# Splitting the gates of a delta rule's decay, and its sums over rows, into high and low halves

## The reference, cut to what matters

```
gc = jnp.cumsum(g, axis=-1)
causal = jnp.tril(jnp.ones((L, L), dtype=bool))
decay = jnp.exp(jnp.where(causal, gc[..., :, None] - gc[..., None, :], -jnp.inf))
a_low = jnp.where(strict, jnp.einsum("bhnid,bhnjd->bhnij", k_beta, k) * decay, 0.0)
...
attn = jnp.where(causal, jnp.einsum("bhnid,bhnjd->bhnij", q, k) * decay, 0.0)
```

## Time and profile before

| | |
|---|---|
| median of 3 runs | 986.37 us (986.13 to 988.43) |
| profiled execution | 986.18 us, span of its instructions 984.4 us |
| PE busy | 973.9 us, 99% |
| POOL busy | 743.1 us, 75% |
| ACT busy | 512.3 us, 52% |
| DVE busy | 364.5 us, 37% |
| mean granted clock of TensorE | 0.998 of full speed |

### The profile page before, as it was taken

The page is one execution under the profiler, slowest core; times in us unless marked ns, Lnnn a source line. Parts: engine busy times, 40 slices in busy tenths (PEclk is TensorE's granted clock), DMA queues, the critical chain, the costliest instruction groups (busy, mean ns, idle before and its releaser), DMA issues.

```text
span 984.4 us, 15403 instructions
## 1 busy us (share of the span) xinstructions
PE 973.9 (99%) x6044; PEld 832.2 (85%) x6044; DVE 364.5 (37%) x842; ACT 512.3 (52%) x759; POOL 743.1 (75%) x593
## 2 busy tenths in 40 slices
PE   9999999999999999999999999999999999999997
PEld 8988889988888888888898887899888888888885
DVE  5686524776524235112111345143252251111103
ACT  6575624465624436456534556485466474444431
POOL 6977633876642998889977888778867789888890
PEclk9999999999999999999999999999999999999999
DMA  7645332545332775667655566555655457666541
GB/s 259 211 140 182 107 109 65 172 150 171 104 113 65 253 241 175 212 187 211 207 158 184 160 209 215 205 172 164 200 175 168 141 168 226 187 183 189 185 134 43
DMA packets 76752, 167.37 MB, mean 170 GB/s; under 512 B 8348, under 2 KB 13704, under 8 KB 76552
## 3 DMA queue, kind: packets, MB, share of 16 engines
q1 hardware_dynamic: 71296, 156.40, 51.6%
q10 hardware_dynamic: 5384, 9.99, 3.2%
HBM read 165.32 MB, written 1.05 MB: 169 GB/s over the span
## 4 chain that ended last, share of the span: by engine, by line
PE 97%; DVE 2%; ACT 0%; DMA 0%; issue 0%; DVEq 0%; ACTq 0%
PE L L517 22%; PE L L519 22%; PE L L518 22%; PE Q L519 2%; PE Q L517 2%; PE Q L518 2%; PE L L889 2%; PE L L890 2%; PE L L891 2%; PE Q L1097 1%; PE Q L734 1%; PE Q L1079 1%; PE Q L1177 1%; PE L L788 1%; PE L L790 1%; PE L L789 1%
## 5 line engine op out<-in xcount | busy, mean ns | idle before, releaser
L504 POOL TENSOR_TENSOR w_lo<-raw,w_hi 128x512 fp32r<-128x512 f32 x588 | 741.6, 1297 | 217.7 <-ACT w_hi L1325 217.0
L1325 ACT CAST w_hi<-raw 128x1024 fp32r<-128x1024 f32 x294 | 305.2, 1054 | 244.8 <-PE L L519 106.4
L517 PE MATMUL L<-w_hi,uH 128*128 128x512 f32 (+1 forms) x768 | 304.4, 396 | 0.3
L519 PE MATMUL L<-w_hi,uL 128*128 128x512 f32 (+1 forms) x768 | 296.4, 386 | 0.0
L518 PE MATMUL L<-w_lo,uH 128*128 128x512 f32 (+1 forms) x768 | 295.9, 385 | 0.0
L517 PEld LDWEIGHTS L<-w_hi,uH 128*128 128x128 f32 x768 | 144.4, 188 | 30.0 <-DVE uL L1944 1.5
L519 PEld LDWEIGHTS L<-w_hi,uL 128*128 128x128 f32 x768 | 144.3, 188 | 29.8
L518 PEld LDWEIGHTS L<-w_lo,uH 128*128 128x128 f32 x768 | 144.6, 188 | 27.1 <-issue 0.5
L517 PE MATMUL L<-w_hi,hH 128*128 128x512 f32 x176 | 69.0, 392 | 0.0
L519 PE MATMUL L<-w_hi,hL 128*128 128x512 f32 x176 | 68.6, 390 | 0.0
L518 PE MATMUL L<-w_lo,hH 128*128 128x512 f32 x176 | 68.5, 389 | 0.0
(11 more groups left out here) (364 smaller groups left out, 1319.9 us busy)
## 6 DMA issues: line engine op xcount, KB each, us to landing
raw<-in_w_in SPq DMA_DIRECT2D x88, 512.0 KB, 3.7
raw<-in_w_ffn_gate SPq DMA_DIRECT2D x22, 512.0 KB, 3.7
raw<-in_w_ffn_up SPq DMA_DIRECT2D x22, 512.0 KB, 3.6
raw<-in_w_ffn_down SPq DMA_DIRECT2D x22, 512.0 KB, 3.6
raw<-in_w_gate SPq DMA_DIRECT2D x22, 512.0 KB, 3.6
raw<-in_w_up SPq DMA_DIRECT2D x22, 512.0 KB, 3.7
raw<-in_w_down SPq DMA_DIRECT2D x22, 512.0 KB, 3.5
raw<-in_w_out SPq DMA_DIRECT2D x16, 512.0 KB, 3.8
```

Source lines behind the costliest of these rows:

```text
L504: last = nc.gpsimd.tensor_tensor(lo[:, cc], raw[:, n % RAW, cc], hi[:, cc].bitcast(F32), ALU.subtract)
L517: mm(dst, sH, wH, start=start, stop=False)
L519: return mm(dst, sL, wH, start=False, stop=stop)
L1325: copy(halves[SLOT[u]][0], raw[:, u % RAW, :]).then_inc(w_hi_there, 1)
```

## The change

The gates g are cast to fp32r (`gH`), and g - `gH` is put into PSUM beside a copy of `gH`. `trg` becomes two tensors, `trgH` from the high halves and `trgL` from the low ones, four products on DVE instead of two. `ones` is cast to an fp32r tensor `onesH` in each `tri` step. On PE the fp32 product of `ones` and `trg` becomes two accumulated fp32r products, `onesH` by `trgH` and `onesH` by `trgL`.

```
-        trg = big("trg", 68, TOKENS)
+        trgH = big("trgH", 68, TOKENS, F32R)
+        trgL = big("trgL", 72, TOKENS, F32R)
+        onesH = big("onesH", 76, [P, P], F32R)
+        gH = big("gH", 76.5, [P, 2 * GH * NT], F32R)
...
                     for t in range(NT):
                         pe.wait_ge(*VE(("tri", gr), t))
-                        mm(Q[t][:], ones, trg[:, t, :, :].rearrange("p h d -> p (h d)"), start=True, stop=True).then_inc(*PE.mark(step, "rows", t))
+                        mm(Q[t][:], onesH[:], trgH[:, t, :, :].rearrange("p h d -> p (h d)"), start=True, stop=False)
+                        mm(Q[t][:], onesH[:], trgL[:, t, :, :].rearrange("p h d -> p (h d)"), start=False, stop=True).then_inc(*PE.mark(step, "rows", t))
...
                 elif kind == "tri":
                     gr = step[1]
-                    gv = Q[2][:, 0:16].rearrange("p (t n) -> p t n", t=NT)[:, :, gr * GH:(gr + 1) * GH]
+                    gv, glv = (Q[2][:, n:n + 16].rearrange("p (t n) -> p t n", t=NT)[:, :, gr * GH:(gr + 1) * GH] for n in (0, 16))
...
-                    v(V.tensor_copy(Q[2][:, 0:16], g))
-                    for t in range(NT):
-                        tt(trg[:, t], each(tri, GH), over(gv[:, t, :], P), ALU.mult, step, t)
+                    v(V.tensor_copy(onesH[:], ones))
+                    v(V.tensor_copy(gH[:], g))
+                    tt(Q[2][:, 16:32], g, gH[:].bitcast(F32), ALU.subtract)
+                    v(V.tensor_copy(Q[2][:, 0:16], gH[:].bitcast(F32)))
+                    for t in range(NT):
+                        tt(trgH[:, t], each(tri, GH), over(gv[:, t, :], P), ALU.mult)
+                        tt(trgL[:, t], each(tri, GH), over(glv[:, t, :], P), ALU.mult, step, t)
```

## The result

The changed kernel takes 988.62 us at the median of 20 runs (988.4 to 992.63), the kernel before 986.45 (986.12 to 989.76, 20 runs). The ratio is 1.0021, 95% interval 1.0015 to 1.0027: 2.2 us slower, against a forecast of 988.7. The profiled execution took 988.95, with a span of 987.1.

What follows compares the result with a forecast made beforehand. PE, busy 99%, was taken to bound the kernel, with DVE's queue full in group 0. DVE's lateness of 3.15 less group 1's gain of 0.80 gave +2.35 us: 988.7 us (+0.24%), range 987.0 to 991.0.

Steps and rivals of the forecast that it cites:

- PE's gain: `rows` products, both groups: four fp32r passes (0.92 us) replace four fp32 passes (1.72); 0.80 us a group, 1.6 in all.
- DVE's work: `tri` step, per group: two casts, the subtraction and two `trgL` products add 2.13 us on DVE without waits.
- the subtraction's wait: Group 0, `tri`: the 16-column subtraction, both operands in SBUF, waits for POOL's running instruction, adding 1.0 us.
- All of it reaches PE: Group 0: DVE's full queue passes its 3.15 us lateness to PE at `tok`; PE's 0.80 is swallowed.
- Where PE waits: Group 0: PE idles some 2.6 us before its first `tok` load, released by DVE's second `decay log`.
- Group 1: Group 1: `gH` and subtraction may wait, taps start 2.6 us late; 3.8 us of slack, so 0.80 is kept.
- The subtraction does wait: Group 0, `tri`: the opposing rival, no wait, had chance 0.15: DVE 2.13 us late, +1.3 us, 987.7.
- The faster case: Rival, chance 0.06: DVE's added work is hidden and nothing is late; -1.6 us, 984.8.
- the second rival: Rival, chance 0.25: in group 0 `gH` waits for POOL as well; DVE 4.3 us late, +3.5 us, 989.9.
- the last rival: Rival, chance 0.04: the granted clock falls during PE's wait in group 0; 2 to 4 us more, 991 to 993.
- The sum: Whole kernel: +3.15 us in group 0 less 0.80 in group 1, +2.35 us, giving 988.7.

Runs made afterwards that it cites:

- group 1 alone: Against the kernel before: the change made in group 1 only, group 0's products left as before; 986.12 us (11 runs), ratio 0.9997.
- the gates in PSUM: Against the changed kernel: g first copied to PSUM, where `gH` and the subtraction read it, one more 16-column copy per group; 989.09 us, ratio 1.0028 to the kernel before.
- the high half twice: Against the changed kernel: no `gH`, subtraction or `trgL`; PE multiplies `onesH` by `trgH` twice; 985.84 us, ratio 0.9990 to the kernel before.
- the kernel with the early tap: Against the kernel before: group 1 changed; in group 0 one tile of third-convolution taps moved earlier, into step `rates`; 985.47 us (12 runs), ratio 0.9990.
- Group 0 alone: Against the kernel before: the change made in group 0's products only, group 1's left as before; 989.81 us (6 runs), ratio 1.0035.

## Why the prediction was right, point by point

- **PE's gain, 0.80 a group: right.** 0.78 to 0.81 in stretch B of the changed kernel, of group 1 alone, of the gates in PSUM and of the high half twice. It counts in group 1 only.
- **DVE's work, 2.13, and the subtraction's wait, 1.0: right.** The terms sum to 3.13 (the forecast wrote 3.15), and 3.11 was measured. The gates read in PSUM separate them: with the wait gone and one small copy more, A falls by 0.86 (0.8 expected).
- **All of it reaches PE and the 0.80 is swallowed: right.** 3.08 in stretch A of the changed kernel, 3.10 with PE's part undone, 0.23 with DVE's part reduced to one cast of 0.26. So even a lateness of a quarter of a microsecond on DVE costs nearly one for one in group 0.
- **Where PE waits: incomplete.** I had "through the wait at L981 and through ACT", with some 2.6 us of idle before the first load of `tok`, released by DVE. It was 0.69 there. The larger idle, 2.56 of the 3.25 between the fill units and `tok`, stands one unit earlier, at the banks that the taps free. I had overlooked this wait, whose mark (taps done) lies 3.3 us before `decay log` and whose place on PE lies 2.7 us before `tok`. The sum was unharmed, because both waits hang on the same DVE queue and the later one ends it.
- **Group 1: right, both in the waits and in the slack.** 2.6 late forecast, 2.59 measured; 0.35 of slack left forecast, 0.39 measured. Tripling `trgL` shows that the slack ends about there.
- **The rivals.** The subtraction does wait, in both groups. The faster case didn't come: the high half twice adds only 0.26 on DVE, and even so group 0 got 0.23 slower and not faster. `gH` waits in group 1 (1.15) and not in group 0 (0.17 to 0.18 in all three kernels with this order there), so the second rival hangs on hundredths of a microsecond between DVE's and POOL's starts, as it said, and didn't happen in any profile of group 0. The Trainium skill ("SBUF — State Buffer", "Who interferes with whom") says that a cast can take the port pair that VectorE shares with GpSimd, and that the order of issue decides which of the two is held up. The trace agrees in both groups. The granted clock stayed full (1.00) through the idles of 1.03 and 2.56 us, so the last rival didn't happen here. It wasn't an empty one: at the start of one execution of the kernel with the early tap the clock did fall, after idles of 1.85 and 1.07 us, with only two transposes between them.
- **The sum.** +2.35 forecast, +2.17 between the medians. The traces give 3.08 - 0.78 = 2.30. That the median came within 0.1 us of the forecast 988.7 is in part luck: the start alone differs by 0.37 between the two profiles, and the medians of the other kernels lay up to 1.2 from what was expected. The mechanism rests on the stretches, not on that.

## What to carry to other kernels

Before giving PE a cheaper form of a product, find who makes its operands and how long that engine has run without a gap when PE next waits for it: here the same edit lost 3.1 us in one group and won 0.8 in the other, and busy shares (PE 99%, DVE 37%) showed nothing of it. A tiny DVE instruction that reads two operands from SBUF, or casts within SBUF, can last 1.15 to 1.23 us when an instruction of POOL (1.30 us) is under way; with one operand read from PSUM it cost 0.17 or 0.18 us. Where a queue has no slack, look first for an idle gap ahead of it into which part of its work can go, and then count again.

## What the runs showed of the hardware that was not expected

That `gH` might wait was foreseen; what the runs add is both outcomes, with times. The cast of 16 columns took 0.17 us in group 0 and 1.15 in group 1 with the same operands, with POOL's instruction starting 0.01 after it in the one case (51.96 and 51.97) and 0.24 before it in the other (198.58 and 198.34). It ended 0.03 after that instruction's record did (199.73 and 199.70). POOL's rows in the timeline of the changed kernel:

```profile
51.97 7.57 POOL L507 TENSOR_TENSOR w_lo<-raw,w_hi 128x512 fp32r<-128x512 f32 x6 [3.00 <-ACT w_hi L1329]
...
198.34 1.36 POOL L507 TENSOR_TENSOR w_lo<-raw,w_hi 128x512 fp32r<-128x512 f32 x1 [1.43 <-ACT w_hi L1329]
```

And `onesH`, eight times as wide, never waited: it was first in both groups. It lasts 0.23 us for 128 columns, less than the 0.3 that the rows of 16 columns (0.18) and 256 (0.48) would suggest. POOL may pay a little for it: its instruction that started 0.02 after `onesH` lasted 1.36 here and with the gates in PSUM, where the mean is 1.30. These are two records, and no run was made to test it.

The fall of the clock at the start of one execution (rows at "Group 1 changed, group 0 with the early tap") was not expected either. In the execution of "Group 0 alone" PE idled 1.44 and 1.07 us at the same place, and the granted clock stayed at 1.00.
